# Products of zeros on TensorE in front of the transposes that follow a norm

## What is computed

```python
def reference(x, ...):
    # first block
    for l in range(2):
        y = token_mixer(x, ...)                 # dilated attention and mLSTM, gated
        x = layer_norm(ALPHA * x + y, ln_g[l, 0], ln_b[l, 0])
        y = swiglu(x, ...) if l == 0 else moe_ffn(x, ...)   # 8 experts, top 2
        x = layer_norm(ALPHA * x + y, ln_g[l, 1], ln_b[l, 1])
    # second block
    for l in range(2):
        p = rms_norm(x, norm_mix_g[l]) @ w_in[l]
        x = x + concat(conformer_conv(p), moba_attention(p), gla(p)) @ w_out[l]
        u = causal_depthwise_conv(rms_norm(x, norm_ffn_g[l]) @ ffn_w_up[l], ...)
        x = x + (silu(u[..., :D_FF]) * u[..., D_FF:]) @ ffn_w_down[l]
    return rms_norm(x, final_g)
```

## Time and profile before

| | |
|---|---|
| median of 3 runs | 2420.73 us (2419.69 to 2421.21) |
| profiled execution | 2413.6 us, of it 2411.8 us from the first to the last instruction |
| TensorE busy | 2286.6 us (95%) |
| VectorE busy | 1750.6 us (73%) |
| ScalarE busy | 1322.5 us (55%) |
| GpSimd busy | 182.3 us (8%) |
| mean granted TensorE clock | 0.966 of full speed |
| DMA | 556.44 MB, mean 231 GB/s |

### The profile page before, as it was taken

The page is one execution under the profiler, slowest core; times in us unless marked ns, Lnnn a source line. Parts: engine busy times, 40 slices in busy tenths (PEclk is TensorE's granted clock), DMA queues, the critical chain, the costliest instruction groups (busy, mean ns, idle before and its releaser), DMA issues.

```text
span 2411.8 us, 41151 instructions
## 1 busy us (share of the span) xinstructions
PE 2286.6 (95%) x16277; PEld 2139.7 (89%) x16277; DVE 1750.6 (73%) x1881; ACT 1322.5 (55%) x1253; POOL 182.3 (8%) x178
## 2 busy tenths in 40 slices
PE   7998999999699999999999999999699999898998
PEld 7998998999689999999999999999588999887997
DVE  4565545457478888888888888888677777667777
ACT  4643443554266767676776777677345444425443
POOL 1000000100000000000000000000390000750000
PEclk9998999999699999999999999999899999879999
DMA  9344655534289999999999999999433555323541
GB/s 303 106 148 133 207 177 170 172 114 159 78 301 340 350 334 349 333 351 353 334 349 332 350 334 351 335 349 341 141 105 115 175 196 175 128 88 122 198 174 56
DMA packets 423432, 556.44 MB, mean 231 GB/s; under 512 B 9746, under 2 KB 377092, under 8 KB 423344
## 3 DMA queue, kind: packets, MB, share of 16 engines
q1 hardware_dynamic: 419232, 544.85, 66.5%
q0 software_dynamic: 4112, 10.38, 1.4%
HBM read 554.13 MB, written 1.06 MB: 230 GB/s over the span
## 4 chain that ended last, share of the span: by engine, by line
issue 46%; PE 42%; DVE 6%; ACT 3%; DVEq 2%; DMA 1%; ACTq 0%; SPq 0%; POOL 0%; POOLq 0%
PE ps L618 12%; PE ps L619 12%; PE ps L620 12%; DVE w_lo L1697 2%; ACT w_hi L1312 2%; PE ps L1188 1%; PE ps L660 1%; DVEq L2164 1%; DVE cvT L2163 0%; PE ps L809 0%; DMA raw<-in_w_in 0%; DVE xn L1733 0%; PE ps L1186 0%; DVE x L1791 0%; PE ps L801 0%
## 5 line engine op out<-in xcount | busy, mean ns | idle before, releaser
L1697 DVE TENSOR_TENSOR w_lo<-raw,w_hi 128x2048 fp32r<-128x2048 f32 x519 | 1180.0, 2284 | 348.6 <-ACT w_hi L1312 347.1
L1312 ACT ACTIVATE w_hi<-raw 128x2048 fp32r<-128x2048 f32 x519 | 987.3, 1909 | 246.6 <-PE ps L620 236.3
L618 PE MATMUL ps<-w_hi,xg_hi 128*128 128x256 f32 x1792 | 515.0, 287 | 9.9 <-DVE xg_lo L2073 7.1
L618 PE MATMUL ps<-xT_hi,w_hi 128*128 128x256 f32 (+1 forms) x1712 | 494.2, 289 | 11.2 <-DVE xT_lo L1707 6.7
L620 PE MATMUL ps<-w_hi,xg_lo 128*128 128x256 f32 x1792 | 503.8, 281 | 0.0
L619 PE MATMUL ps<-w_lo,xg_hi 128*128 128x256 f32 x1792 | 503.3, 281 | 0.0
L619 PE MATMUL ps<-xT_lo,w_hi 128*128 128x256 f32 (+1 forms) x1712 | 489.4, 286 | 0.0
L620 PE MATMUL ps<-xT_hi,w_lo 128*128 128x256 f32 (+1 forms) x1712 | 489.0, 286 | 0.0
L618 PEld LDWEIGHTS ps<-w_hi,xg_hi 128*128 128x128 f32 x1792 | 338.4, 189 | 17.4 <-issue 11.1
L618 PEld LDWEIGHTS ps<-xT_hi,w_hi 128*128 128x128 f32 (+1 forms) x1712 | 332.7, 194 | 16.3 <-issue 8.8
L619 PEld LDWEIGHTS ps<-w_lo,xg_hi 128*128 128x128 f32 x1792 | 338.9, 189 | 4.0
(11 more groups left out here) (442 smaller groups left out, 2795.6 us busy)
## 6 DMA issues: line engine op xcount, KB each, us to landing
raw<-in_exp_w SPq DMA_DIRECT2D x336, 1024.0 KB, 5.6
raw<-in_ffn_w_up SPq DMA_DIRECT2D x44, 1024.0 KB, 5.0
raw<-in_w_in SPq DMA_DIRECT2D x42, 1024.0 KB, 6.9
raw<-in_ffn_w SPq DMA_DIRECT2D x33, 1024.0 KB, 4.9
raw<-in_ffn_w_down SPq DMA_DIRECT2D x22, 1024.0 KB, 5.3
raw<-in_w_gate SPq DMA_DIRECT2D x16, 1024.0 KB, 5.3
raw<-in_w_out SPq DMA_DIRECT2D x8, 1024.0 KB, 4.8
raw<-in_w_o SPq DMA_DIRECT2D x6, 1024.0 KB, 5.6
```

The costliest lines, as they stand in the source:

```text
L618: pe.matmul(out, lhs[0], rhs[0], start=first, stop=False)
L1312: act.activation(w_hi[:, u.const % SPL, 0:width], raw[:, u.const % RAW, 0:width], ACT.Copy)\
L1697: dve.tensor_tensor(w_lo[:, u.const % SPL, 0:width], raw[:, u.const % RAW, 0:width], w_hi[:, u.const % SPL, 0:width].bitcast(F32), ALU.sub ...
```

## The change

At five points of TensorE's program (seven places in time) the kernel now first issues a number of products of zeros, `busy_while_norm(b, n)`: n times a product with 128 columns of `zeros` as weights and its 512 columns as the moving operand, into bank b, each one opening and closing its own sum. They stand right in front of `transpose_x`, behind the last product of the stage before. Their results are read by nobody. `L` is the layer within the block.

```diff
--- before.py
+++ after.py
@@ -660,6 +660,11 @@
                             m = pe.transpose(o[:, c, t, :], src[:, t, (2 * b + c) * P:(2 * b + c + 1) * P], ident)
                     m.then_inc(S_.xT_psum, 1)
 
+            def busy_while_norm(b, n):
+
+                for _ in range(n):
+                    pe.matmul(ps[:, b, :], zeros[:, 0:P], zeros[:], start=True, stop=True)
+
             def open_sums():
 
                 for b in range(4):
@@ -886,6 +891,8 @@
                             m.then_inc(S_.branch_psum, 1)
                     m.then_inc(S_.unit_used, 1)
 
+                if L:
+                    busy_while_norm(4, 17)
                 transpose_x(x, L * 4, 4)
                 T(0, L * 12)
                 T(1)
@@ -960,6 +967,7 @@
                                 m = product(o[t], [v[:, t * P:(t + 1) * P] for v in x_chunks[k]], [v[:, k, :] for v in parts],
                                             k == 0, k == KC - 1)
                     m.then_inc(S_.unit_used, 1)
+                busy_while_norm(7, 17)
                 transpose_x(x, L * 4 + 2, 0)
 
             def router():
@@ -1103,6 +1111,7 @@
 
             def mixer2(L, u):
 
+                busy_while_norm(6, 17 if L else 70)
                 transpose_x(xn, L * 4 + 10, 4)
 
                 def bank_free(n):
@@ -1278,6 +1287,7 @@
                 w_out(1, yA_chunks[2:4])
                 w_out(2, yM_chunks[2:4])
                 w_out(3, yA_chunks[0:2])
+                busy_while_norm(7, 15)
                 transpose_x(xn, L * 4 + 12, 0)
```

## The result

Over 20 runs each, the changed kernel takes 2426.03 us (median; 2415.35 to 2427.82) and the kernel before 2418.41 us (2411.11 to 2421.21). The ratio is 1.0035, with a 95% interval of 1.0025 to 1.0045: slower by 7.6 us in the medians. The profiled execution took 2424.79 us, 2423.0 us of it from the first to the last instruction.

What follows compares the result with a forecast made beforehand. TensorE, busy for 95% of the span, was taken to bound the kernel. Profiled 2413.6 us plus 7.7 for block 2, zero elsewhere, gives 2421.3; with 7.1 carried over, 2428.4 us (+0.32%), own range 2426 to 2432, with rivals 2413 to 2434.

Steps and rivals of the forecast that it cites:

- That the products don't hold the clock: At the seven norms: the clock falls under the added 32-row products as it falls now; forecast's chance 0.50.
- The price at half clock: Each added 512-column product: taken as 0.43 us at half clock, bounded by 0.22 and 0.43; 0.219 at full clock.
- rival C: Half clock costs no more for the added products: no gain, no delay, 2420.7 us; chance 0.04.
- The delay in front of block 2: Block 2, layer 0: 70 products take 27.4 us, transposes start 8.0 us late, 0.3 us comes back: +7.7 us.
- Zero elsewhere: Six other places: no delay, as the zeros fit the gap, VectorE's second half covers them, or the router starts later.
- The base: Profiled execution 2413.6 us; the median of the runs, 2420.73, lies 7.1 us above it, and that is carried over.
- Rival A: Work after 1715 shifts against clock changes; block 2's layer 1 gives the delay back: +2.5, 2423.2 us; chance 0.18.
- its bad side: Block 2's layer 0 narrow products run as slowly as layer 1's: +12.9, 2433.6 us; chance 0.08.
- Rival B: The products hold the clock, so transposes and first products run faster: -7.0 us, 2413.7 us; chance 0.20.

Runs made afterwards that it cites:

- e3: The changed kernel with its counts, but the products of zeros read 128 rows instead of 32; 2413.81 us, ratio 0.9990 to the kernel before.
- e4: The changed kernel with its counts, but the products of zeros read 64 rows instead of 32; 2407.05 us, ratio 0.9953 to the kernel before.
- e5b: The changed kernel with its counts and 32 rows, but products of ones instead of zeros; 2425.14 us, ratio 1.0029 to the kernel before.
- e2: The changed kernel without the 70 products in front of block 2, the 98 elsewhere kept; 2412.36 us, ratio 0.9985 to the kernel before.
- e9: The kernel before plus only 15 products of 128-row zeros per layer of block 2, ahead of gla_out's wait for states; 2399.50 us, ratio 0.9937.
- e6: The changed kernel, 32 rows, with 44 products instead of 70 in front of block 2; 2413.79 us, ratio 0.9994 to the kernel before.

## Why the prediction was right

**That the products don't hold the clock.** Right: the clock falls under the 70 after 3 us, and e3, e4 and e5b show that rows decide and values don't. But the evidence for the step was thin, and part of its coming true is luck. It rested on a single fall in the earlier trace rows and on the earlier trace rows. The fall under L1168 is not the rule. The same 56 products ran to their end at full clock in layer 0 of the same trace, which the prediction doesn't mention, and in layer 1 of the changed kernel; in eleven profiles the clock fell under them in 5 of 22 cases, always in layer 1:

```profile
1769.00:1773.40 4.40, 4.40 (x57) 4.28 (x56) 4.33 (x5) 2.40 (x2) 4.40 (x3) 1.00 0.48 171
2125.40:2129.80 4.40, 4.40 (x57) 4.28 (x57) 4.33 (x5) 2.40 (x2) 4.40 (x3) 1.00 0.49 180
```

(The first line is the kernel before, the second the changed one.) They last 4.5 us; under the 70, over three times as long as that at full clock, it fell in all three kernels that have them with 32 rows. The earlier trace rows was read as if 64 rows were like 32. They are not: 64-row zeros hold a full clock for 15 us (e4), and what narrow work often fails to do is to bring a lost clock back. The forecast did not hang on that. At the three later places of block 2 the 15 or 17 zeros of the changed kernel took 3.4 to 3.8 us and ended before the clock fell.

**The price at half clock.** 0.43 taken, 0.425 measured. The lower bound of 0.22 (rival C) is out.

**The delay in front of block 2.** 27.4 us of zeros forecast, 27.1 measured; transposes 8.0 us late forecast, 7.6 measured against the start of the zeros (8.15 less 0.6). The clock came back with the first product, as supposed. Term +7.7, measured 7.6 by the trace to the first product and 7.3 sixty products on. That the medians too differ by 7.6 is chance beyond some 1.5 us, since each median depends on how the executions fall into the two groups.

**Zero elsewhere.** Right within what the runs can tell: 0.9985 (0.9970 to 1.0001) for e2. In block 1 VectorE's second half covers the zeros, as said.

**The base.** The forecast of 2428.4 is 2.4 us over the measured 2426.03. The median of the kernel before had been 2420.73 over 3 runs and is 2418.41 over 20, and all of the miss is there. The 7.1 us by which the first three runs lay over the profiled execution are the distance of the two groups: the profile was of the lower, the three runs of the upper. Carrying them over took for granted that the changed kernel would lie in its upper group too; 18 of 20 executions do, against 11 of 20 before, and nothing in the prediction says why they should.

**Rival A.** Its mechanism is real. In the profile of the changed kernel its bad side is what happened: +5.3 us in layer 0. In the medians its part isn't known: more of the changed kernel's executions are in the upper group, and no run tells whether the zeros did that. **Rival B** was priced at -7.0. In e3, where the clock does hold, the direct win is 8.8 us, counted until the clock is full in both kernels. For the three later places of block 2 it had 5.5, and 4.9 was won; nothing was won in front of block 2, as it said. In block 1 it had halved 3.1 us for the idle time between the halves of the transposes. That idle time is there (1.75 us), but it lies ahead of the second half, where the win begins, and takes nothing from it: the first two norms alone won 4.0. The half clock behind 424.50, set at about 3.65 us, also lasted 5.1.

## What to carry to other kernels

Filler products that should keep TensorE's clock must read many rows: here the same instruction with 128 rows instead of 32 costs the same time at full clock (0.22 us) and does what it is meant for. Fillers that let the clock fall cost double and stand in the way of the real work. Size a filler for half clock, or look at the granted clock under it, before it goes in front of anything that is on the path. And look for the gap whose lost clock is not won back soon: here that was 2 to 5 us in front of 12 to 23 us of narrow products. The kernel with zeros only there gained 0.63%, the one with the 168 products of 128 rows at the seven norms 0.10% (-0.01 to 0.21).

## What was not expected of the hardware

- 32-row products, back to back, let the clock fall from 2.4 to 1.2 GHz while TensorE is 100% busy: 56 products in 23.8 us at 0.50. 64-row products of the same kind hold it (15.2 us at 1.00 in e4), but in the idle time behind them it falls sooner than behind 128-row ones.
- Narrow work can run to its end without bringing a lost clock back: the same 88 to 89 products, most of them of 64 rows, take 12.45 us at 1.00 (e9) and 22.67 us at 0.50 (layer 0 of e2, e3 and e6). In layer 0 of the kernel before the clock did come back within them (0.74 on the mean, 16.38 us). What went with it in the profiles is when the clock fell, by some tenths of a us.
- The executions of one kernel differ by up to 10 us (2411 to 2421 us for the kernel before), and the longer ones have the lower mean clock. The two kinds of stretches, 5 to 6 us in each layer, are of the size to explain it. Only the profiled execution of each kernel shows its stretches, so for the others this is argued, not shown.
